# Five waits of three steps instead of one ahead of the engines' meeting at the end of retention

## The reference

```
h   = rmsnorm(x, g)
p   = h @ w_in                      # 2048 -> all projected columns
ret = retention(p.ret_q, p.ret_k, p.ret_v)        # group A, returns state S too
sb  = stick_breaking(...)                         # group B
dsa = sparse_attention(...)                       # group C
rw  = rwkv7(...)                                  # group D
x   = x + concat(ret, sb, dsa, rw) * silu(gates) @ w_out
```

```
att = einsum('nqhd,nkhd->nhqk', qc, kc) * dmask
o   = einsum('nhqk,nkhe->nqhe', att, vc) + einsum('nqhd,nhde->nqhe', qc, S) * q_dec
S   = S * s_dec + einsum('nkhd,nkhe->nhde', kc * k_dec, vc)
...
o = o * rsqrt(mean(o * o, axis=-1) + NORM_EPS)    # and S goes out, as p_ret and s_ret
```

## Time and profile before

| | us |
|---|---|
| median of 3 runs | 2989.84 (2989.01 to 2990.37) |
| the profiled execution's own time | 2991.68 |
| its span, first to last instruction | 2989.9 |
| TensorE busy | 2745.0 (92%) |
| VectorE, ScalarE, GpSimd busy | 1489.3, 917.3, 149.0 |

### The profile page before, as it was taken

The page is one execution under the profiler, slowest core; times in us unless marked ns, Lnnn a source line. Parts: engine busy times, 40 slices in busy tenths (PEclk is TensorE's granted clock), DMA queues, the critical chain, the costliest instruction groups (busy, mean ns, idle before and its releaser), DMA issues. The chain is left out here.

```text
span 2989.9 us, 61239 instructions
## 1 busy us (share of the span) xinstructions
PE 2745.0 (92%) x25414; PEld 2536.1 (85%) x25414; DVE 1489.3 (50%) x2604; ACT 917.3 (31%) x1742; POOL 149.0 (5%) x301
## 2 busy tenths in 40 slices
PE   5998999999899997989979989999989999888997
PEld 5997988897787987879979889889877688787997
DVE  4332253336745585963343323532477267589433
ACT  3222253223222342232232223432322215422322
POOL 2100000000011000000002000000000200000001
PEclk7999999999999899989989999999999989998999
DMA  5322334632233222034333233265322422300543
GB/s 177 93 73 73 79 108 113 204 108 72 50 93 86 55 65 88 3 108 136 107 80 91 55 91 97 79 193 155 90 55 54 110 57 76 99 16 13 155 136 126
DMA packets 398474, 277.98 MB, mean 93 GB/s; under 512 B 34460, under 2 KB 368332, under 8 KB 394606
## 3 DMA queue, kind: packets, MB, share of 16 engines
q1 hardware_dynamic: 397278, 263.50, 31.7%
q10 hardware_dynamic: 912, 10.50, 0.9%
HBM read 237.75 MB, written 36.18 MB: 92 GB/s over the span
## 5 line engine op out<-in xcount | busy, mean ns | idle before, releaser
L320 PE MATMUL acc<-h_hi,in_w_hi 128*128 128x272 f32 x3968 | 897.5, 308 | 63.3 <-DVE h_lo L652 35.6
L320 PE MATMUL acc<-h_lo,in_w_hi 128*128 128x272 f32 x3968 | 831.1, 291 | 0.0
L320 PE MATMUL acc<-h_hi,in_w_lo 128*128 128x272 f32 x3968 | 830.1, 291 | 0.0
L320 PEld LDWEIGHTS acc<-h_hi,in_w_hi 128*128 128x128 f32 x3968 | 637.1, 192 | 148.2 <-issue 69.9
L320 PEld LDWEIGHTS acc<-h_lo,in_w_hi 128*128 128x128 f32 x3968 | 635.6, 192 | 0.0
L320 PEld LDWEIGHTS acc<-h_hi,in_w_lo 128*128 128x128 f32 x3968 | 632.0, 192 | 0.0
L350 DVE TENSOR_TENSOR in_w_lo<-in_w_raw,in_w_hi 128x512 fp32r<-128x512 f32 x496 | 346.0, 704 | 422.3 <-ACT in_w_hi L346 419.6
L346 ACT CAST in_w_hi<-in_w_raw 128x512 fp32r<-128x512 f32 x496 | 303.3, 617 | 398.8 <-PE acc L320 311.0
L320 PE MATMUL dr_bank<-over_both,out_weights 128*128 128x272 f32 x1984 | 280.3, 288 | 1.7 <-DVE over_both L691 1.7
L320 PEld LDWEIGHTS dr_bank<-over_both,out_weights 128*128 128x128 f32 x1984 | 260.8, 188 | 1.9 <-DVE over_both L691 1.9
L350 DVE TENSOR_TENSOR out_weights<-regions,out_weights 128x512 fp32r<-128x512 f32 x128 | 88.3, 692 | 182.8 <-ACT out_weights L346 182.7
(11 more groups left out here) (407 smaller groups left out, 3284.2 us busy)
## 6 DMA issues: line engine op xcount, KB each, us to landing
in_w_raw<-in_w_in SPq DMA_DIRECT2D x488, 256.0 KB, 2.9
region<-in_cache_sb_kv SPq DMA_DIRECT2D x128, 256.0 KB, 3.1
regions<-in_w_out SPq DMA_DIRECT2D x128, 256.0 KB, 2.8
regions<-in_cache_dsa SPq DMA_DIRECT2D x64, 160.0 KB, 2.2
region<-x_spill SPq DMA_DIRECT2D x32, 272.0 KB, 3.6
x_spill<-region SPq DMA_DIRECT2D x32, 272.0 KB, 2.1
mix_spill<-mix SPq DMA_DIRECT2D x6, 1088.0 KB, 5.5
mix_back<-mix_spill SPq DMA_DIRECT2D x6, 1088.0 KB, 8.6
```

The costliest lines, as they stand in the source:

```text
L320: last = pe.matmul(self.place(i)[:, c, 0:HALF_N], w[:, u % RING, t, :], part[f][:, HALF_N * c:HALF_N * c + HALF_N], start=first and w is k ...
```

## The change

The last single `yield` of retention on PE, ACT and DVE becomes five. On PE each yields three steps, so 15 steps of the stream stand between the last sum and the meeting, where 3 stood; the 12 steps (three pieces, 72 matmuls) are the first twelve that stood behind the meeting before. The number of instructions is the same on each engine.

```diff
@@ Retention.pe
             last.then_inc(self.summed, 1)
             yield 3
-        yield 3
+        for _ in range(5):
+            yield 3
         meet(pe, self.left, 1)
@@ Retention.act
             act.activation(x, x, ACT.Exp, scale=-0.5).then_inc(self.powered, 1)
             yield
-        yield
+        for _ in range(5):
+            yield
         meet(act, self.left, 1)
```

## The result

The changed kernel takes 2984.78 us (median of 20 runs, 2980.03 to 2991.04), the kernel before 2990.59 us (20 runs, 2986.97 to 2996.23). The ratio is 0.9982, 95% interval 0.9976 to 0.9988: 5.8 us faster by the medians and 5.4 by the ratio, clear of noise and just short of 0.2%. The profiled execution took 2981.68 us, near the low end of the twenty.

What follows compares the result with a forecast made beforehand. TensorE is busy 2745.0 of 2989.9 us, so its stops and slowed clock count. Shorter waits, -0.62 - 0.61 = -1.2 us, with spells unchanged, take the median 2989.84 to 2988.6 us; range 2984 to 2993.

Steps and rivals of the forecast that it cites:

- Who ends the meeting: At the meeting behind retention SP's state stores come last; wait and spell cost 10.9 us per meeting, 21.8 for both.
- The stores move with the steps: On SP's in-order queue the added loads precede the stores, which move back 9.0 us, as TensorE's arrival does.
- The place in the last piece: Before the meeting, VectorE's last subtraction ends 0.62 and 0.61 us earlier against TensorE, cutting the wait from 8.32 to 7.70 us.
- S + 1.60: S is the start on TensorE of the last piece ScalarE awaits before the meeting; VectorE's subtraction ends 1.60 us later.
- The spell behind the wait: TensorE at half clock behind each meeting, 2.6 us lost each time, forecast to stay the same.
- third rival: Different half-clock spells: 2986.4 with 1.1 us less per meeting, 2991.6 or 2998.8 with more; inside the forecast's 0.91 except the last.
- The rest of the span: Outside the meetings nothing was forecast to change: TensorE's sum of work the same, no gain in the sum.
- The stores behind the loads: Second rival: on SP's queue and the DMA engines, added loads delay the stores by 2.1 to 5.8 us; 3000 us, chance 0.04.
- The 17 us spell at the meeting: Half clock for 17 us behind both meetings, 2998.8 us; chance 0.02, shared with a mix with more stops.
- The spread: Launches ran from 2989.01 to 2990.37 us; 1 us was added at both ends for this and the second rival's near end.

Runs made afterwards that it cites:

- stores32: The changed kernel with SP's eight state stores ahead of the three added loads, only the wait for their landing last; 2965.73 us, ratio 0.9917 to the kernel before.
- y2: The changed kernel with two last waits instead of five on TensorE, ScalarE and VectorE, so 3 steps moved; 2987.68 us, ratio 0.9988 to the kernel before.
- pe14: The kernel before with TensorE's last wait of retention 14 steps long instead of 3, the other engines' marks unchanged; 2970.79 us, ratio 0.9941.

## Why the prediction was right, and where it was not

The sign, the range (2984 to 2993) and the mechanism of the wait were right. The size was not: 1.2 us forecast, 5.8 measured. That the time lies in the range is partly luck. The forecast's own range, 2985 to 2992, was missed by 0.2 us, the wider one held with 0.8 us to spare, and most of the gain comes from terms that the sum had at nothing.

*Who ends the meeting.* Right, and shown: the stores on SP. Moving them alone takes 10.7 and 10.8 us out of the two meeting stages, 21.5 together; the forecast had 21.8 for both waits and spells. Its profile is 21.3 us shorter in all, and that execution was the slowest of its five runs; by the medians' ratio the whole kernel gains 24 us, and where the other 2 to 3 us lie no profile shows.

*The stores move with the steps.* Right, shown by the order, by SP's rows, and by stores32, where they don't.

*The place in the last piece.* Right: S + 1.60 as forecast to the hundredth, and a wait of 7.80 and 7.85 us for 7.70. The 0.1 that is missing is in the tail behind the subtraction, 10.11 us for 10.01, which is less than the same kernel's wait varies between profiles. The waits fell by 0.52 and 0.49, together 1.0 us for the forecast's 1.2; in the mean of three profiles of each kernel by 0.65 and 0.47.

*The spell behind the wait.* Here is the first term that was mis-sized. The forecast took "no change", 2.6 us at each meeting; the spells measured 1.55 and 1.95, another 1.7 us won. With the waits that is 2.7 us; by the three profiles of each, the meeting stages are 1.5 and 1.1 us shorter in the middle, 2.6 together. The forecast named a shorter spell as its third rival, with 1.1 us less at each meeting, and set the value by the likeness of the wait. That was the error of reasoning: the wait's length isn't all that sets the spell. In y2 the first wait is 8.34 us as in the kernel before, and the spell behind it is another:

```profile
277.19 0.66 PE L320 MATMUL acc<-h_hi,in_w_lo 128*128 128x272 f32 x2
277.65 0.47 PE L320 MATMUL acc<-h_hi,in_w_hi 128*128 128x272 f32 x2
277.96 0.41 PE L320 MATMUL acc<-h_lo,in_w_hi 128*128 128x272 f32 x2
```

Six pairs from 274.76 to 277.65, 2.89 us where 1.5 would do: 1.4 us lost, not 2.6, and y2's first meeting stage is 1.1 us shorter. What sets the length of a spell instead, no run shows.

*The rest of the span.* This is the second mis-sized term, and the larger one. The forecast let the spells elsewhere be as they are, with a few us of room. In the three profiles of each kernel the stretch between the meeting stages is 2.7 us shorter (1350.5 for 1353.2 in the mean) and the one behind the second 2.8 us (1169.9 for 1172.7), though no work in them was changed. With the 2.6 us of the meeting stages and the 1.3 us ahead of the change that makes the 9.4 us by which the spans differ. The timed medians differ by 5.8, so the three executions lie on the fast side of the changed kernel's runs (2981.6 to 2982.6 us in a spread of 2980 to 2991), and how much of the 5.8 each stretch has in the mean of the runs isn't settled. That untouched work supplies about half of it is what 5.8 less 2.6 says, a subtraction and not a measurement.

The timed runs agree with the clock as the carrier. Of the changed kernel's twenty, the nine with a mean granted clock of 0.958 or 0.959 took 2980.0 to 2984.6 us, and the nine with 0.954 to 0.956 took 2984.7 to 2991.0. Its median is 0.957; that of 27 runs of the kernel before is 0.955. A mean that is 0.002 higher over 2985 us stands for 12 us less at half clock; at 0.45 us lost in each of them while TensorE is busy that is 5.4 us, an estimate, and the clocks are rounded to 0.001, so it can be 3 us off either way. Why the moved steps leave fewer spells behind them stays open.

*The rivals.* The stores behind the loads: not seen. The four loads ahead of the stores take 8.78 us, so they came at the stream's pace and not in a burst, and the landing took 0.1 us more. The 17 us spell at the meeting: not seen either.

*The spread.* The forecast took the launches' spread from three runs, 1.4 us. Twenty runs of the same kernel spread over 9.3 us.

## What to carry to other kernels

Where engines meet, look for the one that comes last and for what stands before the meeting in its own queue. Work moved in front of the meeting covers nothing while the late one moves along with it; moving eight stores to where their data was ready was worth four times the 12 steps. When a profile shows spells of lower clock, two kernels can differ by some microseconds in work that was not changed. Split the span at the same instructions of both kernels, see that no cut falls into a spell, and profile each more than once, before naming a cause for a difference of that size.

## What the runs showed of the hardware that was not expected

Work that no edit touched takes different times, repeatably by kernel: between the two meeting stages the kernel before took 1352.8 to 1353.5 us in three profiles and the changed one 1350.0 to 1350.9, with the same instructions. The spells at half clock lie otherwise: around the end of the sparse group one unbroken spell of 27 us stands in the one, and in the other a spell that is interrupted for 3.2 us, with one more (1011.4 to 1018.0 us) behind it. A cut inside such a spell makes the difference look larger, 4.6 us. What decides between the two was not found.

At pe14's second meeting a wait of 2.25 us was enough to be followed by a spell (1.6 us lost), and at its first one of 1.82 us was not.
